# A half-width triangular solve: each level computes only the 32 of 64 columns that it changes

## The reference, cut to what matters

```python
def step(state, inp):                      # run once forwards and once backwards over the 256 tokens
    r_t, w_t, k_t, v_t, a_t, b_t = inp
    sa = jnp.einsum('dbhvk,dbhk->dbhv', state, a_t)
    state = (state * w_t[..., None, :] + sa[..., :, None] * b_t[..., None, :]
             + v_t[..., :, None] * k_t[..., None, :])
    return state, jnp.einsum('dbhvk,dbhk->dbhv', state, r_t)
```

## Time and profile before

| | |
|---|---|
| median of 3 runs | 1642.8 us (1632.86 to 1642.88) |
| profiled execution | 1646.6 us, its span 1644.7 us |
| TensorE busy | 1560.4 us, 95% of the span |
| VectorE busy | 1174.0 us, 71% |
| ScalarE busy | 760.6 us, 46% |
| GpSimd busy | 90.1 us, 5% |
| mean granted TensorE clock | 0.982 of full speed |

### The profile page before, as it was taken

How to read it: one execution, slowest core, us unless ns; L and a number is a source line. 1 busy time by engine, 2 the same in 40 slices (tenths; PEclk the granted TensorE clock), 3 DMA queues, 4 the chain that set the end, 5 groups by cost and what they waited for, 6 DMA issues and landing times.

```text
span 1644.7 us, 40178 instructions
## 1 busy us (share of the span) xinstructions
PE 1560.4 (95%) x17083; PEld 1444.8 (88%) x17083; DVE 1174.0 (71%) x1739; ACT 760.6 (46%) x1169; POOL 90.1 (5%) x103
## 2 busy tenths in 40 slices
PE   6999999998898999999999999999989989999999
PEld 6999897777788899999899999868788888999998
DVE  4777776787886576777666766769887765777764
ACT  5444564465161345444444445545721613554442
POOL 1000120000030001000100001200000300010000
PEclk9999999899999999999999999989998999999999
DMA  5855542232011345655556555323320213566554
GB/s 179 274 181 182 190 141 90 78 116 78 17 61 47 104 154 169 194 185 185 191 197 230 185 187 179 116 65 116 103 67 16 73 35 103 156 182 193 187 183 153
DMA packets 61940, 227.92 MB, mean 139 GB/s; under 512 B 6896, under 2 KB 7920, under 8 KB 60880
## 3 DMA queue, kind: packets, MB, share of 16 engines
q1 hardware_dynamic: 60624, 218.26, 41.1%
q0 software_dynamic: 1152, 7.21, 1.2%
HBM read 224.69 MB, written 1.05 MB: 137 GB/s over the span
## 4 chain that ended last, share of the span: by engine, by line
PE 76%; DVE 13%; ACT 5%; issue 3%; DMA 2%; ACTq 0%; SPq 0%; DVEq 0%; POOLq 0%
PE banks L568 16%; PE banks L570 15%; PE banks L569 15%; PE banks L634 10%; PE banks L635 5%; DVE wlo L1516 3%; PE banks L979 2%; DVE cvx L1766 2%; DMA raw<-in_stream 2%; ACT whi L1139 2%; DVE arena L1993 1%; PE banks L860 1%; ACT arena L1334 1%; PE banks L746 1%; PE banks L991 1%
## 5 line engine op out<-in xcount | busy, mean ns | idle before, releaser
L1516 DVE TENSOR_TENSOR wlo<-raw,whi 128x1024 fp32r<-128x1024 f32 x411 | 506.4, 1235 | 298.9 <-ACT whi L1139 297.6
L1139 ACT CAST whi<-raw 128x1024 fp32r<-128x1024 f32 x411 | 429.4, 1048 | 465.4 <-PE banks L570 318.9
L568 PE MATMUL banks<-hx,whi 128*128 128x256 f32 x1696 | 487.0, 287 | 21.3 <-DVE wlo L1516 17.4
L569 PE MATMUL banks<-hx,whi 128*128 128x256 f32 x1696 | 481.3, 284 | 0.0
L570 PE MATMUL banks<-hx,wlo 128*128 128x256 f32 x1696 | 481.2, 284 | 0.0
L568 PEld LDWEIGHTS banks<-hx,whi 128*128 128x128 f32 x1696 | 326.7, 193 | 28.3 <-DVE wlo L1516 16.8
L569 PEld LDWEIGHTS banks<-hx,whi 128*128 128x128 f32 x1696 | 326.9, 193 | 0.2
L570 PEld LDWEIGHTS banks<-hx,wlo 128*128 128x128 f32 x1696 | 326.8, 193 | 0.0
L634 PE MATMUL banks<-gg,whi 128*128 128x512 f32 x704 | 244.3, 390 | 0.0
L568 PE MATMUL banks<-h,whi 128*128 128x256 f32 x760 | 230.5, 303 | 9.9 <-ACT arena L1237 5.4
L569 PE MATMUL banks<-h,whi 128*128 128x256 f32 x760 | 219.4, 289 | 0.0
(11 more groups left out here) (298 smaller groups left out, 1912.5 us busy)
## 6 DMA issues: line engine op xcount, KB each, us to landing
raw<-in_stream SPq DMA_DIRECT2D x411, 512.0 KB, 3.5
arena<-in_wuq POOLq DMA_DIRECT2D x2, 1152.0 KB, 11.7
lo_w<-in_lora POOLq DMA_DIRECT2D x2, 1024.0 KB, 7.9
arena<-in_wukv POOLq DMA_DIRECT2D x2, 1024.0 KB, 14.9
xT<-in_x SPq DMA_DIRECT2D x1, 1024.0 KB, 4.9
out<-xT SPq DMA_DIRECT2D x8, 128.0 KB, 3.4
consts<-in_cst SPq DMA_DIRECT2D x1, 642.5 KB, 8.4
masks<-in_msk POOLq DMA_DIRECT2D x1, 288.0 KB, 4.0
```

Source lines behind the costliest of these rows:

```text
L568: TE.matmul(o, wh, hi, start=first, stop=False, **kw)
L569: TE.matmul(o, wh, lo, start=False, stop=False, **kw)
L1139: SE.copy(whi[:, m % HL, :], raw[:, m % RAW, :]).then_inc(hi_ready, 1)
L1516: TT(wlo[:, m % HL, :], raw[:, m % RAW, :], whi[:, m % HL, :].bitcast(F), ALU.subtract)\
```

## The change

Every level changes only half of the columns of each 64x64 block: in level `lv`, with s = 2 to the power lv, those groups of s columns whose number is odd or even, by direction and orientation (`wing`, `wings`). The change computes, masks and subtracts only these.

- TensorE: every product of the levels reads a moving operand of 32 columns instead of 64 and writes 32 columns. The number of products and their weights (64 columns) stay.
- The two orientations are now stored so that `mn[:, 0]` and `mn[:, 1]` hold the same orientation on both halves of the partitions (masks and the turned products are laid accordingly).
- VectorE: the masks of level 0 (128x512) and the identity's addition (128x1024) take half of the elements, and so do the masks of `z` (128x512 to 128x256) and the subtractions (128x1024 to 128x512; in the last level one orientation alone, 128x256).
- GpSimd: `clear_zz` zeroes the other half of `zz` ahead of level 1 (2 memsets of 128x256), and after `mz` of levels 1 to 4 that part of the old half which the next level doesn't write (2 memsets of 128x128 for a level). `mz` waits for them. `clear_zz(0)` stands in GpSimd's program behind the convolution's padding and ahead of its mean, `clear_zz(1)` behind its last work for the convolution (L549) and ahead of `norm(2)`.
- ScalarE: two copies of the identity's columns (128x512 each) into `mn` ahead of the pairs; VectorE's addition waits for them.

```diff
+            def clear_zz(d):
+                pool.wait_ge(*ten.at(("turned pairs", d, 1)))
+                settled(pool)
+                for q in QUADS:
+                    other = zz[:, 4 * q:4 * q + 4].rearrange("p x t (n b s) -> p (x t n) b s", b=2, s=2)[:, :, 1 - d, :]
+                    nc.gpsimd.memset(other, 0.0).then_inc(*poo.mark(("zz cleared", d, q, 1)))
+                for lv in range(1, LEVELS - 1):
+                    for q in QUADS:
+                        pool.wait_ge(*ten.at(("mz", d, q, lv)))
+                        settled(pool)
+                        old = zz[:, 4 * q:4 * q + 4].rearrange("p x t (n B b s) -> p (x t n) B b s", B=2, b=2, s=2 ** lv)
+                        nc.gpsimd.memset(old[:, :, 1 - d, d, :], 0.0).then_inc(*poo.mark(("zz cleared", d, q, lv + 1)))
...
+                clear_zz(0)
...
+                clear_zz(1)
...
+                        for x, t, i, e, f in both:
+                            o = (x * NT + t) * HALF_C
+                            m = TE.matmul(bank[3 * q][f, o:o + HALF_C].rearrange("p (n s) -> p n s", s=s),
+                                          g1[e, 4 * q + x, t, 0, :], wing(mn[e, 0, 4 * q + x, t, :], s, d),
+                                          start=True, stop=True)
...
+                        pe.wait_ge(*poo.at(("zz cleared", d, q, lv)))
+                        pe.wait_ge(*vec.at(("z", d, q, lv)))
...
+                            if lv < LEVELS - 1:
+                                TE.matmul(bank[3 * q + 1][e, o].rearrange("p (n s) -> p n s", s=s), m_t, wing(z_, s, d),
+                                          start=True, stop=True)
+                            m = TE.matmul(bank[3 * q + 2][f, o].rearrange("p (n s) -> p n s", s=s), z_, wing(m_t, s, 1 - d),
+                                          start=True, stop=True)
...
+                    for i in range(2):
+                        b = (1 - d, d)[i]
+                        m = SE.copy(mn[:, i].rearrange("p x t (n b) -> p (x t) n b", b=2)[:, :, :, b],
+                                    cc("ident64", C).rearrange("p (n b) -> p n b", b=2)[:, :, b].unsqueeze(1)
+                                    .broadcast_to([P, H * NT, HALF_C]))
+                    m.then_inc(*act.mark(("eye", d)))
...
-                            TT(zz[:, 4 * q:4 * q + 4].rearrange("p x t n -> p (x t) n"),
-                               bank[3 * q].rearrange("p (x n) -> p x n", n=C), mask, ALU.mult)\
+                            TT(zz[:, 4 * q:4 * q + 4].rearrange("p x t (n b s) -> p (x t) n b s", b=2, s=s)[:, :, :, d, :],
+                               bank[3 * q][:, 0:S].rearrange("p (x n s) -> p x n s", n=HALF_C // s, s=s), mask, ALU.mult)\
...
-                            m4 = mn[:, :, 4 * q:4 * q + 4].rearrange("p i x t n -> p i (x t n)")
-                            TT(m4, m4, banks[:, 3 * q + 1:3 * q + 3, :], ALU.subtract)\
-                                .then_inc(*vec.mark(("mn", d, q, lv)))
+                            m4 = wings(d, q, s)
+                            p4 = banks[:, 3 * q + 1:3 * q + 3, 0:S].rearrange("p i (n s) -> p i n s", s=s)
+                            if lv == LEVELS - 1:
+                                m4, p4 = m4[:, 1], p4[:, 1]
+                            TT(m4, m4, p4, ALU.subtract).then_inc(*vec.mark(("mn", d, q, lv)))
```

More of the change, by code:

```diff
@@ L171, in constants @@
             if n == 0:
-                m1[:C, d, 0], m1[C:, d, 0], m1[:C, d, 1], m1[C:, d, 1] = -1.0 * m, -1.0 * m.T, -1.0 * m.T, -1.0 * m
+                m1[:, d, 0], m1[:, d, 1] = two(-1.0 * m), two(-1.0 * m.T)
             else:
@@ L395, in program, with wing, wings @@
         zz = view(M0 + 6 * Q1, H, NT, C)
+        HALF_C = C // 2
+        def wing(a, s, b):
+            return a.rearrange("p (n b s) -> p n b s", b=2, s=s)[:, :, b, :]
+        def wings(d, q, s):
+            n, one = H * NT * C, 4 * NT * C
+            m, m_t = (0, s) if d == 0 else (s, 0)
+            at = MN + q * one + m
+            pair = arena[:, at:at + 2 * (n + m_t - m)].rearrange("p (i n) -> p i n", i=2)[:, :, 0:one]
+            return pair.rearrange("p i (n b s) -> p i n b s", b=2, s=s)[:, :, :, 0, :]
         ys = view(M0 + 7 * Q1, H, NT, HD)
@@ L963, in _ @@
                             b_, k_k = bt[r:r + HD, j, t * P + e * C:t * P + (e + 1) * C], kr4[r:r + HD, j, t, 1 - e, :]
-                            w = bank[4 + x % 4 // 2][:, S * e + o:S * e + o + C]
+                            w, w_t = (bank[4 + x % 4 // 2][:, n + o:n + o + C] for n in (0, S))
                             TE.matmul(w[HD * e:HD * e + HD, :], k_k, b_, start=True, stop=True)
-                            m = TE.matmul(w[HD - HD * e:P - HD * e, :], b_, k_k, start=True, stop=True)
+                            m = TE.matmul(w_t[HD - HD * e:P - HD * e, :], b_, k_k, start=True, stop=True)
                         m.then_inc(*ten.mark(("turned pairs", d, q)))
@@ L973, in _, with z_products @@
                             for x in range(4) for t in range(NT) for i in range(2)]
+                    def z_products(q, lv):
+                        s = 2 ** lv
+                        pe.wait_ge(*vec.at(("g2", d, 1) if lv == 1 and q == 0 else ("mn", d, q, lv - 1)))
+                        settled(pe)
+                        for x, t, i, e, f in both:
[3 more added lines that the diff above has]
+                                          start=True, stop=True)
+                        m.then_inc(*ten.mark(("z", d, q, lv)))
@@ new lines, in mz_products @@
+                    def mz_products(q, lv):
+                        s = 2 ** lv
+                        pe.wait_ge(*poo.at(("zz cleared", d, q, lv)))
+                        pe.wait_ge(*vec.at(("z", d, q, lv)))
+                        settled(pe)
+                        for x, t, i, e, f in both:
+                            o = slice((x * NT + t) * HALF_C, (x * NT + t + 1) * HALF_C)
+                            m_t, z_ = mn[f, 1, 4 * q + x, t, :], zz[f, 4 * q + x, t, :]
+                            if lv < LEVELS - 1:
[3 more added lines that the diff above has]
+                                          start=True, stop=True)
+                        m.then_inc(*ten.mark(("mz", d, q, lv)))
@@ L974, in _ @@
                     for lv in range(1, LEVELS):
                         for q in QUADS:
[L976 to L980, removed]
@@ L981, in _ @@
-                            m.then_inc(*ten.mark(("z", d, q, lv)))
+                            z_products(q, lv)
                         fr.at(("level", d, lv))
                         for q in QUADS:
[L984 to L992, removed]
@@ L993, in _ @@
-                            m.then_inc(*ten.mark(("mz", d, q, lv)))
+                            mz_products(q, lv)
                     for q in QUADS:
@@ L1007, in _ @@
                                     m = TE.matmul(bank[3 * q + 1][e, (x % 4 * NT + t) * C:(x % 4 * NT + t + 1) * C],
-                                                  mn[f, i, x, t, :], tk[f, 0, t, h * HD:(h + 1) * HD],
+                                                  mn[f, 1, x, t, :], tk[f, 0, t, h * HD:(h + 1) * HD],
                                                   start=True, stop=True)
@@ L1016, in _ @@
                                     m = TE.matmul(bank[3 * q + 2][e, (x % 4 * NT + t) * C:(x % 4 * NT + t + 1) * C],
-                                                  mn[f, i, x, t, :], gv[f, x, t, :], start=True, stop=True)
+                                                  mn[f, 1, x, t, :], gv[f, x, t, :], start=True, stop=True)
                         m.then_inc(*ten.mark(("y", d, q)))
@@ L1957, in _ @@
                         ve.wait_ge(*ten.at(("turned pairs", d, q)))
[L1958 to L1963, removed]
+                        for i in range(2):
+                            b = (d, 1 - d)[i]
+                            TT(mn[:, i, quad].rearrange("p (e j) t (n b) -> p e (j t) n b", e=2, b=2)[:, :, :, :, b],
+                               banks[:, 4:6, i * S:(i + 1) * S].rearrange("p e (x n b) -> p e x n b", n=HALF_C, b=2)[:, :, :, :, b],
+                               m1[:, i].rearrange("p (n b) -> p n b", b=2)[:, :, b].unsqueeze(1).unsqueeze(1)
+                               .broadcast_to([P, 2, 4, HALF_C]), ALU.mult).then_inc(*vec.mark(("m%d" % i, d, q)))
                         TT(g2[:, quad].rearrange("p x t i n -> p x t (i n)"),
@@ L1966, in _ @@
                             .then_inc(*vec.mark(("g2", d, q)))
-                        mn4 = mn[:, :, quad].rearrange("p i x t n -> p i (x t) n")
+                        mn4 = wings(d, q, 1).rearrange("p i (x n) s -> p i x (n s)", n=HALF_C)
+                        one4 = one.rearrange("p (n b) -> p b n", b=2)
+                        one4 = (one4 if d == 0 else one4[:, ::-1]).unsqueeze(2).broadcast_to([P, 2, 4 * NT, HALF_C])
                         ve.wait_ge(*vec.at(("m0", d, q)))
                         ve.wait_ge(*vec.at(("m1", d, q)))
```

(11 more changed lines are left out.)

## The result

The change made the kernel **slower**, by 1.6%: 1665.1 us (median of 4 runs, 1661.6 to 1668.3) against 1642.8 us, a ratio of 1.016 (95% interval 1.012 to 1.020). The profiled execution took 1661.6 us, 15.0 more than the profiled one of before.

A forecast was written before the change was run, and what follows sets the result against it. The solves were taken as bound by VectorE and TensorE alternating, then by instruction supply. Two layers of 4.3 us forward and 1.7 backward gave 12.0 us off 1642.8, rounded to 1631 us; range 1617 to 1646.

The forecast's parts named there:

- What bounds the kernel: In the solves, VectorE and TensorE take turns on the path; the supply of instructions is the second bound.
- The path of a forward level: In the forward solves, a level's chain of subtraction, z, mask and taps falls from 5.99 to 5.09 us.
- the 5.64 us: Forward level's floor from instruction supply: 195 pairs, 1.52 packets at 3.7 us each, whatever the engines do.
- the 5.2: Check on forward levels: if they drop under 5.2 us, the supply of instructions was misread.
- VectorE's operations: Solve masks and subtractions: strided halves cost the same per element; a subtraction loses 0.53 us, a mask 0.27.
- rival D: Nothing arrives: strided halves cost as much as the whole, or the gain is waited for behind the solve; 1640 to 1645, chance 0.16.
- GpSimd and ScalarE at nothing: GpSimd's clears and ScalarE's two copies in the solves lie beside other work and cost 0.
- The 10 us beside it: Possible cost if each of a solve's 8 clears slowed a subtraction by 0.32 us; taken as 0.
- TensorE's products at no change: In the solves' levels, products of 32 columns keep the pace of 64, since weight loads set it.
- The clock: TensorE's granted clock in the solves: a fall held possible, but 80% busy had kept it high in the trace.
- Rival E: Slower: narrower products leave the array emptier and the clock falls within the solves; 1666 us if half the levels, chance 0.08.
- The range: Whole kernel: 1617 to 1646 us, leaving out the falling clock and the case of matmuls halving too.

The follow-up runs named there:

- run 1: The changed kernel with z and mz products streaming 64 columns again, all else as changed: 1630.8 us, ratio 0.993 to the kernel before.
- run 6: As run 1, but a quarter of the mz products left out from level 2 on (wrong results): 1612.0 us, ratio 0.984.
- run 7: As run 1, but each GpSimd clear preceded by one of the same size into a spare place: 1629.5 us, ratio 0.994.
- run 8: As run 1, plus blocks of unneeded products of one form each ahead of gv in the backward direction: 1640.8 us, single run.

## Why the prediction was wrong

**What bounds the kernel**: right in its two parts, with the second put too strongly. The path of a forward level was forecast at 5.09 us; first levels of the changed kernel took 5.0 while its clock was up, and run 1 has levels of 5.07 and 5.14. The same levels fall under the 5.64 us that a level could not be shorter than, and under the 5.2 that was to show the supply as misread. As a bound of every single level it is refuted; as one of the mean it stands: a level takes 5.8 on average in both forward solves of run 1, and run 6 brings them down by leaving instructions out.

**VectorE's operations**: right. Strided halves cost by their elements, 0.69 and 0.42 us. That excludes the first of rival D's two conditions, and the 10.5 us that arrive in run 1 speak against the second.

**GpSimd and ScalarE at nothing**: right for GpSimd, by run 7. The 10 us beside it, for subtractions slowed by clears, were too low by their own row (0.57 us and not 0.32, and 10 clears a solve), but nothing of the kind came: 128x512 takes 0.69 us throughout. ScalarE's copies were not tested by themselves; run 1 has them and still gains 10.5 of the 12.0.

**TensorE's products at no change**: right at full clock, and for the reason given, the weight loads (run 8). The MATMUL instruction did not get 26 ns shorter either: 217 ns against 221 in run 8. At half clock narrow products are hardly faster than wide ones: 64 narrow `z` pairs go at 53 ns each there (3.6 us for a level's), the wide ones of the earlier trace rows at 56 ((2.61 - 0.3) over 41 steps), while VectorE's waits of a microsecond in the timeline above show that the path is all TensorE's.

**The clock**: this is the step that failed. The sum was made at the clock of the earlier trace rows, 0.95 to 1.00, and it was 0.59 to 0.70. Rival E, which names the mechanism that came, got 0.08. The argument against it was that waits get shorter and that the clock had been 1.00 in three solves of four. The second half took a property of the 64-column products for one of the stage. The first half does not tell the two kernels apart. Here are the first 9.0 us of the first solve, in the changed kernel (up to the fall of the clock) and in run 1 (where it stays up to the end of the solve):

```profile
408.40:417.40 9.00, 7.98 (x286) 7.38 (x290) 6.57 (x14) 0.00 (x0) 0.44 (x2) 1.00 0.18 64
405.00:414.00 9.00, 7.87 (x272) 7.14 (x276) 6.31 (x13) 0.00 (x0) 0.45 (x2) 1.00 0.19 64
```

TensorE is busy for as long, with about as many products; only their width differs. I had computed that narrow products run at the pace of wide ones, and did not ask what the clock makes of the same busy time with half of the columns. What it answers to is not shown beyond that: the runs show that width decides here, not by what rule.

A row of the kernel before, right behind its third solve, could have warned that a busy TensorE does not keep the clock up:

```profile
1260.30:1277.40 17.10, 17.10 (x159) 14.18 (x158) 5.46 (x10) 3.28 (x9) 0.00 (x0) 0.50 0.06 23
```

These 17.1 us at half clock have no idle TensorE and no 32-column product in them. So narrow products are one way to half clock and not the only one.

The 11.60 us at a clock of 0.50 hold no idle TensorE at all. The Trainium skill's "TensorE: Matmul & The Clock Gate", section "What's actually happening", lists the 1.2 GHz level as that of an idle or cold engine; the trace does not agree with it here, where idle is read as the profile's busy time has it, and the measurement decides.

How the sizes add up: without the clock the change is worth 10.5 us (run 1; forecast 12.0). Between the profiled executions of run 1 and of the changed kernel, 26.3 of the 29.9 us lie in the solves and 3.4 ahead of the first one; the products right behind the solves start at half clock, but what they lose is won back elsewhere. The medians differ by 34 us.

Rival E's price of 1666 us, measured 1665, was in part luck. It took ten of the 20 levels at half clock, each 3.5 us longer. A forward level there takes 7.91 us against 5.8 in run 1, 2.1 longer, and some twelve levels ran so (an estimate from the half-clock time in the solves, about 100 us): 25 us in place of 35. What makes up the rest of the 34 us between the medians is not shown.

**The range** (1617 to 1646) left E out as one of two cases of 0.08. The sign of the outcome hung on it.

## What to carry to other kernels

When a matmul is limited by its weight load, halving the columns it streams saves no time on TensorE, and can cost the clock: ask of every narrowing what the granted clock was in that stage with the wide products and whether anything guarantees it with the narrow ones. Let TensorE compute columns that nobody reads if they are free, and cut the work where it costs, at the engine that empties PSUM. And a rival that nearly doubles the time of a product in a whole stage deserves a place in the range, unless a row excludes it.

## What the runs showed of the hardware

- The clock stayed at 0.50 over 11.60 us in which TensorE was busy all the time, with 32-column products; in all four solves it fell 8 to 13 us after the first product, in the second or third level. It rose again 2.5 to 4.6 us after the end of the solve, during products of 64 columns. The kernel before had 17.1 us at 0.50 with a busy TensorE and no narrow product.
- Weight loads slow down with the clock: the mean load of `z` was 135 ns in the first level, at full clock, and 223 ns in the levels at half clock. A pair of narrow `z` products took 29 ns and 53 ns.
- One kind of narrow product alone cost 5 to 6 us by the medians, about the scatter of the runs; both together cost 34.
- Instructions arrive in packets of 128 pairs: 135 packets for 17083 pairs, 131 with 448 pairs fewer in run 6, 139 with 512 more in run 8. In the first solve of run 1 they lie 3.4 to 4.3 us apart, 3.8 on average. A stage of short products (15 to 29 ns a pair) can be bound by that.
